# An encoder block on one core: the convolution branch's output projection as seven block products

## What is computed

```python
attn = _mla_attention(q_n, q_r, k_n, k_r, v).reshape(B, L, N_HEADS * V_DIM) @ w_o_attn[l]
...
c = lax.conv_general_dilated(a * jax.nn.sigmoid(b), conv_w[l][:, None, :], ...) + conv_b[l]
c = jax.nn.silu(_layernorm(c, conv_ln_g[l], conv_ln_b[l]))
conv = c @ w_conv_out[l]                      # 768 tokens, 1024 x 1024
...
h = h + (g_a * attn + g_c * conv) @ w_out[l]  # 1024 x 1024
u = _rms(h, norm_mlp[l])
h = h + jnp.square(jax.nn.relu(u @ w_mlp_in[l])) @ w_mlp_out[l]   # 1024 x 4096, 4096 x 1024
return _rms(h, norm_final)[:, N_META:]
```

## Time and profile before

| | |
|---|---|
| three runs | 1244.51, 1250.12, 1248.03 us, median 1248.03 |
| the profiled execution | 1247.35 us, span of its instructions 1245.8, granted clock 0.997 |
| PE busy | 1212.9 us (97%) |
| DVE, ACT, POOL busy | 899.0, 553.6, 430.4 us |
| stage U_CO (637.8 to 705.6) | 67.8 us, PE busy throughout |
| stage U_OUT (705.6 to 763.9) | 58.3 us, PE busy throughout |

### The profile page before, as it was taken

How to read it: one execution, slowest core, us unless ns; L and a number is a source line. 1 busy time by engine, 2 the same in 40 slices (tenths; PEclk the granted TensorE clock), 3 DMA queues, 4 the chain that set the end, 5 groups by cost and what they waited for, 6 DMA issues and landing times.

```text
span 1245.8 us, 18362 instructions
## 1 busy us (share of the span) xinstructions
PE 1212.9 (97%) x6797; PEld 1077.4 (86%) x6797; DVE 899.0 (72%) x1043; ACT 553.6 (44%) x814; POOL 430.4 (35%) x299
## 2 busy tenths in 40 slices
PE   6999999999999999999999999999999999999997
PEld 5888888888888889987888888999999988887886
DVE  4115999999986666675664765576759796677887
ACT  6234211222245666674352445544653244445555
POOL 2454433488855555464744163000120000002101
PEclk9999999999999999999999999999999999999999
DMA  6347988899899797967897333334693343438633
GB/s 193 94 135 158 203 197 178 201 236 240 182 257 230 171 224 176 277 103 182 202 216 241 110 106 119 119 122 132 163 210 133 120 152 121 134 127 209 177 130 118
DMA packets 174369, 211.70 MB, mean 170 GB/s; under 512 B 13039, under 2 KB 125741, under 8 KB 174300
## 3 DMA queue, kind: packets, MB, share of 16 engines
q1 hardware_dynamic: 136300, 155.19, 40.0%
q0 software_dynamic: 35696, 49.29, 24.3%
q10 hardware_dynamic: 2304, 6.29, 1.3%
HBM read 201.31 MB, written 88.08 MB: 232 GB/s over the span
## 4 chain that ended last, share of the span: by engine, by line
PE 76%; issue 7%; DMA 5%; POOL 5%; DVE 3%; ACT 3%; SPq 1%; POOLq 0%; ACTq 0%; DVEq 0%
PE psum L528 32%; PE psum L2386 17%; PE psum L2365 15%; PE psum L2335 4%; DMA raw<-in_w_mlp_in 3%; PE psum L2188 2%; POOL wlo L515 2%; PE psum L2218 1%; PE psum L2061 1%; POOL lnacc L1981 1%; DMA wsums<-in_w_mlp_out 1%; PE psum L2200 1%; DMA raw<-in_w_mlp_out 1%; POOL isums L1894 0%; DVE olo L1528 0%
## 5 line engine op out<-in xcount | busy, mean ns | idle before, releaser
L515 POOL TENSOR_TENSOR wlo<-raw,whi 128x1024 fp32r<-128x1024 f32 (+1 forms) x72 | 167.7, 2330 | 200.3 <-ACT whi L510 200.1
L1369 DVE SCALAR_TENSOR_TENSOR psum<-cs,convw,psum 128x799 f32<-128x799 f32 x196 | 189.5, 1052 | 0.0
L528 PE MATMUL psum<-uhi,whi 128*128 128x512 f32 x592 | 152.5, 338 | 0.8 <-POOL wlo L515 0.8
L528 PE MATMUL psum<-uhi,wlo 128*128 128x512 f32 x592 | 153.0, 339 | 0.0
L528 PE MATMUL psum<-ulo,whi 128*128 128x512 f32 x592 | 152.6, 339 | 0.0
L510 ACT ACTIVATE whi<-raw 128x1024 fp32r<-128x1024 f32 (+1 forms) x73 | 72.1, 987 | 108.8 <-PE psum L528 98.2
L528 PEld LDWEIGHTS psum<-uhi,whi 128*128 128x128 f32 x592 | 91.4, 188 | 14.7 <-POOL wlo L515 1.6
L528 PEld LDWEIGHTS psum<-uhi,wlo 128*128 128x128 f32 x592 | 91.7, 188 | 12.9
L528 PEld LDWEIGHTS psum<-ulo,whi 128*128 128x128 f32 x592 | 91.5, 188 | 12.5
L2365 PE MATMUL psum<-u2hi,rawlo 128*128 128x384 f32 x304 | 102.2, 336 | 0.0
L2365 PE MATMUL psum<-u2hi,whi 128*128 128x384 f32 x296 | 99.9, 338 | 2.1 <-DVE rawlo L1764 2.0
(11 more groups left out here) (291 smaller groups left out, 3112.0 us busy)
## 6 DMA issues: line engine op xcount, KB each, us to landing
raw<-in_w_in SPq DMA_DIRECT2D x38, 512.0 KB, 4.5
isums<-in_w_mlp_in SPq DMA_DIRECT2D x32, 512.0 KB, 7.8
isums<-in_w_mlp_in POOLq DMA_DIRECT2D x32, 512.0 KB, 8.1
wsums<-in_w_mlp_out SPq DMA_DIRECT2D x32, 512.0 KB, 10.7
wsums<-in_w_mlp_out POOLq DMA_DIRECT2D x32, 512.0 KB, 10.8
raw<-wsums SPq DMA_DIRECT2D x22, 512.0 KB, 3.2
raw<-isums SPq DMA_DIRECT2D x20, 512.0 KB, 3.3
raw<-in_w_mlp_in SPq DMA_DIRECT2D x18, 512.0 KB, 3.8
```

Source lines behind the costliest of these rows:

```text
L515: gp.tensor_tensor(out=wlo[:, c % 2, 0:w], in0=raw[:, c % 4, 0:w], in1=whi[:, c % 2, 0:w].bitcast(F32), op=ALU.subtract).then_inc(lo_ready, 1)
L528: mm = nc.tensor.matmul(out[:, o0:o0 + n], a, b[:, k, c0:c0 + n], start=first and step == 0, stop=last and step == 2)
L1369: ins = nc.vector.scalar_tensor_tensor(out=out, in0=src, scalar=w, in1=a, op0=ALU.mult, op1=ALU.add)
```

## The change

`w_conv_out` is computed as seven block products. A unit is now one product (of seven) for half of an output half, 256 columns (J), over 512 inputs and 384 tokens: 24 matmuls of 384 columns; 14 units. Sums of products that two results share stay in PSUM: three pairs of banks X, Y, Z, where ScalarE copies an intermediate sum (`co_hold` to `xheld`, `zheld`) before the next product is added to it, and VectorE adds product and held copy, multiplies by the gate block and adds to `zacc` (`co_drain`, four for each J). The tokens' blocks T1 to T4 are sums that VectorE makes (`c_mix`). The weights' sums lie in HBM (`csums`, four, each made by one copy and one addition, where numbers 1 and 3 start from 0 and 1); `osums` are made the same way, so that copies 1 and 3 wait for sums 0 and 1.

```diff
+CO_MIX = (
+    dict(a=((0, 0),), b=(0, 0), banks="X", new=True),
+    dict(a=((0, 1),), b=(1, 0), banks="Y", new=True),
+    dict(a=((1, 0), (1, 1), (0, 0)), banks="X", new=False),
+    dict(a=((1, 0), (1, 1)), banks="Z", new=True),
+    dict(a=((0, 0), (1, 0)), banks="X", new=False),
+    dict(a=((1, 0), (1, 1), (0, 0), (0, 1)), b=(1, 1), banks="Z", new=False),
+    dict(a=((1, 1),), banks="X", new=False),
+)
...
+            for v in range(CO_UNITS):
+                J, p = v // 7, v % 7
+                wh, wl = ring_weights(U_CO + v, KD // 2)
+                if v == 1:
+                    pe.wait_ge(merged, KD)
+                if p == 1 and J == 1:
+                    pe.wait_ge(gated, 1)
+                if p == 2:
+                    pe.wait_ge(co_held, 3 * J + 1)
...
+                if p == 6:
+                    pe.wait_ge(gated, 7 * J + 3)
...
+                for k in range(KD // 2):
...
+                    for e in range(2):
+                        for step, (a, b) in enumerate(((wh, chi), (wh, clo), (wl, chi))):
+                            mm = nc.tensor.matmul(bank[:, 2 * co_pair(J, p) + e, 0:THIRD], a[:, k, e * P:(e + 1) * P], b[p][:, k, :],
...
+            def co_drain(J, e):
+
+                half, tokens, p = CO_BLOCKS[e]
+                n, done = 4 * J + e, 7 * J + 2 * e
+                held = (xheld, zheld, xheld, None)[e]
...
+                if held is not None:
+                    dve.wait_ge(co_held, 3 * J + (1, 3, 2)[e])
+                    nc.vector.tensor_tensor(out=gconv[:, :, :], in0=pair_banks(co_pair(J, p)), in1=held[:, :, :], op=ALU.add).then_inc(gated, 1)
...
+                nc.vector.tensor_tensor(out=gconv[:, :, :], in0=gconv[:, :, :] if held is not None else pair_banks(co_pair(J, p)), in1=gate,
+                                        op=ALU.mult).then_inc(gated, 1)
...
+                nc.vector.tensor_tensor(out=made, in0=made, in1=gconv[:, :, :],
+                                        op=ALU.add if half == 0 else ALU.subtract).then_inc(merged, 1)
```

```diff
+            def ring_free(n):
+
+                if n < U_RING + 4:
+                    sp.wait_ge(lo_ready, n - 3)
+                elif n < U_RING + RING:
+                    sp.wait_ge(unit_used, U_RING - 1 + n % 2)
+                else:
+                    sp.wait_ge(unit_used, n - RING + 1)
...
-                if x < RING:
-                    sp.wait_ge(unit_used, U_OUT + max(u for u in range(OUT_UNITS) if u % RING == x) + 1)
-                else:
-                    sp.wait_ge(unit_used, U_IN + x - RING + 1)
-                sp.dma_start(x_place(x), x_block(x, 0)).then_inc(m_landed[x % RING], 16)
+                ring_free(U_IN + x)
+                sp.dma_start(x_place(x), x_block(x, 0)).then_inc(m_landed[place(U_IN + x)], 16)
...
+            for n in range(U_CO, U_IN):
+                if n not in VECTOR_UNITS:
+                    gp.wait_ge(hi_ready, n + 1)
+                    gp.tensor_tensor(out=mlo[place(n)], in0=mraw[place(n)], in1=mhi[high(n)].bitcast(F32),
                                      op=ALU.subtract).then_inc(lo_ready, 1)
+                if n in (U_CO + 5, U_CO + 6):
+                    block_sum_add(2 * (n - U_CO - 5), 1)
+                if n == U_CO + 11:
+                    block_sum_add(1, 1)
+                if n == U_OUT + 2:
+                    block_sum_add(3, 1)
```

More of the change, by code:

```diff
@@ L177, with co_pair, place, high @@
 OUT_SUMS = tuple(x["b"] for x in OUT_MIX if len(x["b"]) > 1)
[L179 to L183, removed]
+Z_MIXED = ((S1, 0), (S2, 0), (S3, 0), (S4, 0), (S1, 1), (S2, 1), (S3, 1), (S4, 1))
+Z_HIGHS = ((0, 0), (S1, 0), (0, 1), (S2, 0), (S3, 0), (S4, 0), (1, 0), (S1, 1), (S2, 1), (S3, 1), (1, 1), (S4, 1), (6, 0), (6, 1))
+Z_LOWS = ((0, 0), (S1, 0), (0, 1), (S2, 0), (S3, 0), (S4, 0), (1, 0), (1, 1), (S1, 1), (S2, 1), (S4, 1), (S3, 1), (6, 0), (6, 1))
 Z_SLOTS = (0, 1, 2, 3, 4, 5, 0)
[L187 to L194, removed]
+CO_MIX = (
[7 more added lines that the diff above has]
+)
+T2, T1, T3, T4 = 2, 3, 4, 6
+CO_SUMS = (CO_MIX[3]["a"], CO_MIX[2]["a"], CO_MIX[4]["a"], CO_MIX[5]["a"])
+CO_BLOCKS = ((0, 0, 1), (1, 1, 4), (0, 1, 5), (1, 0, 6))
+C_MIXED = tuple((p, part) for p in (T1, T2, T4, T3) for part in range(2))
+C_HIGHS = tuple((p, part) for p in (0, 1, T1, T2, T4, T3, 5) for part in range(2))
+C_LOWS = C_HIGHS
+def co_pair(J, p):
+    return {"X": (3, 0)[J], "Y": 1, "Z": 2}[CO_MIX[p]["banks"]]
+U_RING = U_CO
+VECTOR_UNITS = (U_CO + 1, U_CO + 2)
+def place(n):
+    return (n - U_RING) % 6
+def high(n):
+    return (n - U_RING + 1) % 3
+def landed(n):
+    return 16 * ((n - U_RING) // 6 + 1 + (U_RING // 4 if place(n) < 4 else 0))
 MIXES = len(MIX)
@@ L773, in gate_back, with gate_block @@
                 sp.dma_start(gin[:, g % 2], gates[g]).then_inc(gin_landed[g % 2], 16)
[L775 to L783 removed]
+            def gate_block(n):
+                half, tokens, _ = CO_BLOCKS[n % 4]
+                first = KD + 4 * half + n // 4 * 2
+                sp.wait_ge(merged, KD + n - 1)
+                sp.dma_start(gblock[:, n % 2], gates[first:first + 2, :, tokens * THIRD:(tokens + 1) * THIRD]
+                             .rearrange("a p n -> p a n")).then_inc(gin_landed[n % 2], 16)
@@ new lines, in _ @@
+            block_sum_copy(0, 0), block_sum_copy(2, 0)
+            for g in range(KD + 3):
+                if g < KD:
+                    columns(w_o, U_O + g - g % 4, 0, g % 4, slice(g * P, (g + 1) * P))
+                else:
+                    co_load(g - KD)
+                if g == 2:
+                    block_sum_copy(1, 0)
+                if g >= 3:
+                    gate_back(g - 3)
+                if g == 7:
+                    block_sum_copy(3, 0)
+            for v in range(3, CO_UNITS):
+                co_load(v)
+                if v in (3, 4):
+                    gate_block(v - 3)
+                if v in (6, 7):
+                    block_sum_copy((v - 6) * 2, 1)
+                if v == 8:
+                    gate_block(2)
+                    sp.wait_ge(c_lo, len(C_LOWS))
@@ L1594, in _ @@
+            gate_attn(0)
+            for j in range(KD):
+                centre(range(j, j + 1))
+                if j > 1:
+                    ln_sq_add(j - 1)
+                if j == 3:
+                    gate_attn(1)
+            ln_sq_add(KD - 1)
+            gate_attn(2), gate_attn(3)
             dve.wait_ge(ln_root, 1)
```

446 lines of the change are left out of this document (262 added, 184 removed).

## The result

The changed kernel takes 1254.44 us at the median (1250.46 to 1260.51, 14 runs), the kernel before 1247.59 (1243.39 to 1253.68, 14 runs); the ratio is 1.0052 with a 95% interval of 1.0036 to 1.0068. The forecast was 1255 and slower by a little over half a per cent. The profiled execution of the changed kernel took 1255.08 us with a span of 1253.5.

What follows compares the result with a forecast made beforehand. TensorE, working in 97% of the span, was taken to bound the kernel. From the profiled 1247.35 us, -9.5 - 4.5 + 5 + 6 + 10.5 = +7.5 gave 1255 us, range 1238 to 1263.

Steps and rivals of the forecast that it cites:

- Fewer matmuls: In the w_conv_out stage: 336 matmuls of 384 columns at 0.1734 us take 58.3 us instead of 67.80, -9.5.
- The start of `w_mlp_in`: After w_out: first block loaded four units earlier, so a 2.63 us pause and 1.84 of lower clock go, -4.5.
- The start of the stage: At w_conv_out's start: VectorE's added work makes product 1 wait 2.8 us, product 2 1.2, plus 1 for clock, +5.
- Product 9: In w_conv_out: its weights load behind h1 with two additions running; pause 4.3 us and 1.7 for clock, +6.
- The two bounds: When product 9's data come: 671 without a pause, or 681 if queues share DMA engines; value taken nearer the upper.
- Product 13 and the start of `w_out`: VectorE, late, meets GpSimd remainders: product 13 pauses 5.5 us, clock 1.5, w_out's first two units 3.5, +10.5.
- rival (a): Product 9's weights come in time, at 671 to 676, and VectorE never gets behind: 1240 us, faster; chance 0.31.
- At nothing: Copies and additions for w_conv_out, ScalarE's holds, loads in longer rows, and order for w_out and x_hi: no cost.
- Rival (b): Product 9 pauses, but VectorE meets three remainders, not five or six, so product 13 doesn't: 1245 us; chance 0.15.

Runs made afterwards that it cites:

- e10: Changed kernel with h1 later in SP's queue, VectorE and ScalarE work ordered by need, GpSimd remainders up to w_out's fourth unit zero-filled: 1237.79 us, ratio 0.9919.
- e7: Kernel before, only with w_mlp_in's blocks in another order of places, so the first loads after w_out's unit 8: 1244.42 us, ratio 0.9968.
- e1: Changed kernel with h1's two transfers moved in SP's queue from behind product 8's load to behind w_out's third load: 1247.19 us, ratio 0.9994.
- e2: Changed kernel with the first two additions for osums (1 MB each) cut to one block of 128 columns: 1244.3 us in one run.
- e9: Changed kernel with VectorE and ScalarE work ordered by need, h1 in the place the change gave it: 1252.55 us, ratio 1.0045.
- e3: Changed kernel with GpSimd zero-filling the low parts of the weights of products 3 to 13 instead of subtracting: 1251.0 us in one run.

## Why the prediction held, point by point

1. *Fewer matmuls, -9.5.* The stage is busy for 64.20 us; 5.8 of that are the lower clock (worked out below with the same 0.1734), which leaves 58.4 for a term of 58.3. e10 shows it without that: the clock is 1.00 through its whole stage, and TensorE is busy for 58.5 of 59.0 us. By the formula of the Trainium skill ("TensorE: Matmul & The Clock Gate", section Back-to-back issue gap) that is quoted there it would have been 54.6; the traces go with the row.

2. *The start of `w_mlp_in`, -4.5.* No pause, 4.19 us for the 24 matmuls instead of 6.00. e7 shows it alone, -3.9.

3. *The start of the stage, +5.* Pause 2.22 us, and 14.35 us for the next 72 matmuls instead of 72 x 0.1734 = 12.48: 2.22 + 1.87 = +4.1. VectorE met a remainder twice (3.17 and 3.15 us), not three times. Product 2 didn't wait: the lower clock behind product 1 gave its bank copy, which ended at 646.30, the time until 647.43.

4. *Product 9, +6.* Pause 7.02, clock 10.25 - 48 x 0.1734 = 1.93: +9.0. The mechanism was right (e1, e2, e9); the term was under-sized by 3 us. That the landing at 680.18 is near the forecast 681 is chance, since the stage began 2.8 us before the 637.8 of the forecast, and h1 with it. Counted from the stage's first matmul, h1 went out when forecast (19.4 us for 19.7), but from there to the landing took 25.7 us and not 23.5 (the 1.3 for landing in that sum have no row behind them), and product 9 was due 0.7 us sooner, as part 3 cost less. The two bounds were 671 and 681; e2 shows that without the additions the load comes in time. The median of 4.1 us for small loads beside additions, which the prediction held against the sharing, was the milder of two rows: the view behind the earlier trace rows has 7.0 us for three loads of `w_conv_out`.

5. *Product 13 and the start of `w_out`, +10.5.* Pause 4.77, clock 6.18 - 4.16 = 2.0, and U_OUT 61.0 for the 58.5 that it takes without pauses (e7): +9.2. The size was about right, and half of the reason. `w_out`'s pauses came at its third and fourth unit, not at the first two. That VectorE meets GpSimd's remainders five times ahead of the drain is in the trace and shown by e3 and e10 (from 682.84 to the end of the drain's first step 24.1 us, for a forecast of 23.6 to 25.6):

```profile
682.84 0.96 DVE L1801 TENSOR_TENSOR gconv<-psum,gblock 128x768 f32<-128x768 f32 x1 [13.16 <-DMA gblock<-gates]
683.83 3.00 DVE L1804 TENSOR_TENSOR zacc<-zacc,gconv 128x768 f32<-128x768 f32 x1
...
690.47 3.16 DVE L1849 TENSOR_TENSOR zsum<-zsum,zacc 128x768 f32<-128x768 f32 x1
693.55 3.59 DVE L1849 TENSOR_TENSOR zsum<-zacc 128x768 f32<-128x768 f32 x1
697.06 3.16 DVE L1856 TENSOR_TENSOR zlo<-zsum,zhi 128x768 fp32r<-128x768 f32 x1
700.15 3.15 DVE L1856 TENSOR_TENSOR zlo<-zacc,zhi 128x768 fp32r<-128x768 f32 x1
...
706.01 0.95 DVE L1798 TENSOR_TENSOR gconv<-psum,zheld 128x768 f32<-128x768 f32 x1
```

But the pause doesn't need product 9's (e1), and what held VectorE before 682.84 was a gate block in the same queue, not ScalarE's copy of product 7's bank, which was done at 681.96 and which VectorE came to at 687.62. The prediction, its rival (a) too, let the one follow from the other; they are two causes.

6. *At nothing.* The copies and additions for `w_conv_out` and the squares on VectorE show no wait of TensorE in `w_o_attn`'s stage. That they cost nothing was not tried by itself.

The sum of the measured terms is -9.5 - 4.5 + 4.1 + 9.0 + 9.2 = +8.3, for +7.7 between the two profiled spans. Two shifts lie outside the terms: the stage began 2.6 us earlier (first matmul at 635.03 for 637.62; 1.6 of it stood already in attention, where the same group of matmuls begins at 527.17 for 528.77), and a pause of `w_mlp_in` near 938 us, 1.94 in one piece instead of 2.0 in two, let the clock fall (24 matmuls in 6.04 us), which costs 1.9. That the forecast of +7.5 comes within a microsecond of all this is partly luck: parts 3 and 5 were too large by 0.9 and 1.3, part 4 too small by 3.0.

Rival (a), 1240 with the data in time, is what e2 looks like (1244.3 in one run): its condition, the landing in time, decides product 9's pause as described. But its sum left 1.5 us for parts 4 and 5 together, and e2 still has 2.2 us before product 13, a clock of 0.74 behind that and 60.7 us of U_OUT for 58.5. Rival (b) needed no more than three meetings ahead of product 13's drain; there were five.

## What to carry to other kernels

Where a stage bound by TensorE gets fewer matmuls but more work on the other engines, work out for each queue what now stands ahead of the load that comes due first, and count a large transfer there together with every addition that runs beside it. A step of VectorE with two SBUF operands should be priced at two lengths, alone and beside a GpSimd operation that reads, and the count of the second is what decides when a drain is due; and GpSimd's step too, where it falls into a run of such VectorE steps. Look for the cheap part of a change by itself: here the seam to the next stage, a few index expressions, is worth as much as the whole change in its best order.
